# MoE layers of a hybrid decoder trunk: stored expert results cleared in advance, loaded two steps sooner, and the last two steps' results added on the chip

## The chip, the cores and the metric

The kernel runs on one core of a Trainium2 chip. The metric is the time of one execution on the device in microseconds (us). Each core has five engines: TensorE (PE; its weight loads are listed as PEld), VectorE (DVE), ScalarE (ACT), GpSimd (POOL) and SyncE (SP), which here only issues DMAs.

## What is computed

512 tokens of width 1024 in float32 pass through two layers, each with a mixer and a mixture of experts (MoE) in post-norm form, `x <- LN(alpha*x + mixer(x)); x <- LN(alpha*x + MoE(x))`. Layer 0 has an S5 and convolution mixer, layer 1 a sparse attention. The change is in the MoE, which is the same in both layers:

```python
def moe(x, router_w, router_b, w_gate, w_up, w_down, s_gate, s_up, s_down):
    scores = jax.nn.sigmoid(xt @ router_w)
    _, idx = lax.top_k(scores + router_b, TOP_K)          # 8 of 64 experts
    gate = jnp.take_along_axis(scores, idx, axis=1)
    gate = gate / gate.sum(-1, keepdims=True) * ROUTE_SCALE
    ...
    def expert_rows(args):
        tok, g, e = args
        xb = x_pad[tok]
        h = jax.nn.silu(xb @ w_gate[e]) * (xb @ w_up[e])  # 1024 -> 256
        return (h @ w_down[e]) * g[:, None]               # 256 -> 1024
    ...
    routed = jnp.zeros((n + 1, d), x.dtype).at[row_tok].add(y_rows.reshape(n_rows, d))[:n]
    shared = (jax.nn.silu(xt @ s_gate) * (xt @ s_up)) @ s_down
    return (routed + shared)
```

Each token's output is thus the sum of 8 gated expert rows and the shared expert's row; 512 x 8 = 4096 expert rows in all.

## The kernel before, in words

`program` calls `even_mixer`, `moe_layer` 0, `odd_mixer`, `moe_layer` 1. Each is a block with one instruction stream per engine; the streams wait for each other through semaphores only, and each stream runs in the order in which it is written. There is a barrier between blocks.

`moe_layer` has three stages.

*The start* (PE from L479, DVE from L708). The mixer's output projection (`out_project`), the first norm, the router and the shared expert run tile by tile (4 tiles of 128 tokens). SP loads constants and shared weights (L222 to L227), then stores each normed tile to `h_dram` (L229 to L231) as it comes, then the second norm's constants, and once the routing is known, the first experts' weights (L235 on). POOL fills tables, and gathers rows only after all four stores have landed (L329).

*The steps.* A step handles 128 rows. Three steps `k` = 0, 1, 2 make a round `t`; steps 0 and 1 serve one expert each, step 2 two experts with 64 rows each. POOL gathers the rows' inputs from `h_dram` (`gather`, L300), PE turns them (`rows_transposes`, L421), multiplies with gate and up weights (`gate_up`, L439 and L442), turns the hidden rows (L452) and multiplies with the down weights (`down`, L472 and L475). ACT and DVE scale one half each by the gates into `y[k]` (`scale`, L652 and L785), and POOL scatters `y[k]` to `y_dram`, row 8 x token + rank (`send`, L315). Places of a step that no token fills have an index beyond the bounds and are not written. Every step of a round but the last also starts weight loads on SP (L268 to L281). One step comes ahead of the rounds (t = -1, k = 2); the loop over `t` has a last round of its own, written out. Here there are 49 steps in each layer.

*The tail.* SP waits until all three steps of the last round are scattered (L250 to L253) and then loads all of `y_dram`, 16 loads of 1 MB, each two of the eight rows of 128 tokens, into `pieces`, 16 places in `wide`, `weights` and `xy` (L124, L283 to L286). Tile by tile, DVE adds rows 0 to 2 to `x` (`add_row`, L898), PE adds rows 3 to 7 in PSUM by matmuls with the identity (`row_sums`, L578, 10 matmuls, each listed as two records), DVE adds that sum (the "fold", L906) and runs the norm (L1001 to L1011). In layer 0, PE also turns the result into `g.xT` (`turn_output`, L587) for the next part, and SP loads the next part's `wide` weights when tile 0 is folded (L288). In layer 1 SP stores the tiles to `out` (L293).

## Time and profile before

| | us |
|---|---|
| median of 3 runs | 2124.73 |
| lowest, highest | 2122.98, 2125.33 |
| the profiled execution | 2123.23 |
| its span | 2121.2 |
| PE busy | 1990.8 (94%) |
| DVE busy | 746.5 (35%) |
| ACT busy | 400.1 (19%) |
| POOL busy | 394.7 (19%) |
| DMA, bytes moved | 566.01 MB, mean 267 GB/s |

The span runs from the first to the last instruction of the profiled execution; its time, 2123.23 us, holds 2 us more around it. Busy shares overlap, and matmuls are pipelined, so a busy PE is not one at its peak. Layer 0's MoE block runs from about 210 to 993 us, layer 1's from about 1341 to the end. A timeline's row merges neighbours of one kind: it gives the start of the first, the time from it to the end of the last, and their count; idle time ahead of it stands in brackets with what ended it. `PEclk` is the clock that TensorE was granted, as a share of 2.4 GHz (0.50 is 1.2 GHz).

### The profile page before, as it was taken

What the parts mean: (1) busy time and instruction counts of PE and PEld (TensorE: products, weight loads), DVE (VectorE), ACT (ScalarE), POOL (GpSimd) and SP (SyncE); (2) the same over time, 40 slices, a digit from 0 to 9 for tenths busy, and PEclk for the clock granted to TensorE, in tenths of its full rate; (3) what the DMA queues carried; (4) which work ended last, traced back from release to release, by engine and by line L of the source; (5) the groups of instructions that cost most, each with busy time, mean ns of one, the idle gap of its engine ahead of it and who ended that gap; (6) DMA issues with size and microseconds to landing.
All of it is one profiled execution on the core that took longest, in us unless ns stands there. A gap on an engine that the chain in (4) does not pass through costs nothing. (4 is left out here: it accounts for less than half of the span.)

```text
span 2121.2 us, 26424 instructions
## 1 busy us (share of the span) xinstructions
PE 1990.8 (94%) x8534; PEld 989.3 (47%) x8534; DVE 746.5 (35%) x1929; ACT 400.1 (19%) x890; POOL 394.7 (19%) x381
## 2 busy tenths in 40 slices
PE   8998998999999999978998898998999999999977
PEld 4553454444444444433446565554444444444433
DVE  3683352222222222216432566343222222222216
ACT  2103021111111111101002566111111111111110
POOL 0000200111111111100110778500111111111110
PEclk9999999999999999999998899999999999999998
DMA  6132245999999999958402000226899999999957
GB/s 227 11 53 113 111 190 212 400 407 412 406 409 388 412 396 386 401 229 352 78 0 80 1 2 2 105 77 266 334 407 402 417 406 411 399 412 400 406 220 332
DMA packets 107426, 566.01 MB, mean 267 GB/s; under 512 B 38625, under 2 KB 39393, under 8 KB 69089
## 3 DMA queue, kind: packets, MB, share of 16 engines
q1 hardware_dynamic: 79136, 497.99, 59.1%
q0 software_dynamic: 28224, 67.16, 8.1%
q8 instruction: 40, 0.66, 0.1%
q14 instruction: 26, 0.20, 0.0%
HBM read 539.78 MB, written 59.77 MB: 283 GB/s over the span
## 5 line engine op out<-in xcount | busy, mean ns | idle before, releaser
L439 PE MATMUL moe_bank<-moe_weights,moe_xgT 128*128 128x512 f32 x1024 | 457.0, 599 | 15.5 <-DMA moe_weights<-in_ex_weights 15.1
L439 PEld LDWEIGHTS moe_bank<-moe_weights,moe_xgT 128*128 128x128 f32 x1024 | 190.0, 190 | 232.2 <-issue 215.9
L315 POOL DMA_INDIRECT y<-moe_xy,moe_rows x98 | 98.6, 1006 | 945.2 <-DVE moe_idx L757 569.1
L777 DVE TENSOR_TENSOR moe_hid<-moe_sil,moe_bank 128x256 f32<-128x256 f32 x98 | 41.3, 421 | 661.1 <-ACT moe_sil L640 661.1
L472 PE MATMUL moe_bank<-moe_weights,moe_hidT 128*128 128x512 f32 x512 | 230.5, 593 | 0.0
L442 PE MATMUL moe_bank<-moe_weights,moe_xgT 128*64 128x512 f32 x512 | 226.6, 595 | 0.0
L442 PE MATMUL moe_bank<-wide,moe_xgT 128*64 128x512 f32 x512 | 226.6, 595 | 0.0
L640 ACT ACTIVATE moe_sil<-moe_bank 128x256 f32<-128x256 f32 x98 | 37.6, 383 | 657.4 <-PE moe_bank L439 456.0
L785 DVE TENSOR_SCALAR moe_xy<-moe_bank,moe_sgate 128x512 f32<-128x512 f32 x98 | 73.6, 751 | 219.5 <-PE moe_bank L472 142.1
L300 POOL DMA_INDIRECT moe_xy<-h,moe_idx x98 | 99.9, 1019 | 267.1 <-DVE moe_idx L757 239.5
L1847 POOL TENSOR_SCALAR att_prob<-att_prob,att_coef 128x128 f32<-128x128 f32 (+3 forms) x128 | 136.7, 1089 | 60.6 <-DVE att_coef L2015 37.8
L472 PEld LDWEIGHTS moe_bank<-moe_weights,moe_hidT 128*128 128x128 f32 x512 | 92.4, 191 | 93.4 <-issue 93.4
L421 PEld LDWEIGHTS moe_bank<-const_sb,moe_xy 128*128 128x128 f32 x784 | 100.6, 192 | 67.5 <-issue 51.6
L442 PEld LDWEIGHTS moe_bank<-moe_weights,moe_xgT 128*64 128x64 f32 x512 | 67.5, 137 | 128.8 <-issue 127.9
L652 ACT ACTIVATE moe_xy<-moe_bank,moe_sgate 128x512 f32<-128x512 f32 x98 | 67.3, 687 | 290.9 <-PE moe_bank L472 190.7
L348 PE MATMUL moe_bank<-wide,xT 128*128 128x512 f32 x256 | 113.7, 600 | 7.7 <-PEq L46 7.7
L475 PE MATMUL moe_bank<-moe_weights,moe_hidT 128*64 128x512 f32 x256 | 116.7, 598 | 1.9 <-ACT moe_hidT L644 1.9
L475 PE MATMUL moe_bank<-wide,moe_hidT 128*64 128x512 f32 x256 | 116.7, 598 | 0.0
L421 PE MATMUL moe_bank<-const_sb,moe_xy 128*128 128x128 f32 x784 | 107.5, 281 | 9.7 <-DMA moe_xy<-h,moe_idx 9.7
L348 PEld LDWEIGHTS moe_bank<-wide,xT 128*128 128x128 f32 x256 | 48.3, 193 | 65.0 <-issue 65.0
L1953 ACT ACTIVATE att_prob<-att_prob,att_low 128x128 f32<-128x128 f32 (+3 forms) x128 | 70.4, 551 | 33.7 <-DVE att_low L1979 33.6
L770 DVE COPY moe_xgT<-moe_bank 128x512 f32<-128x512 f32 x98 | 67.8, 692 | 18.4 <-PE moe_bank L421 18.0
(353 smaller groups left out, 2432.8 us busy)
## 6 DMA issues: line engine op xcount, KB each, us to landing
moe_weights<-in_ex_weights SPq DMA_DIRECT2D x96, 2048.0 KB, 19.6
moe_weights<-in_ex_weights SPq DMA_DIRECT2D x96, 1024.0 KB, 19.2
wide<-in_ex_weights SPq DMA_DIRECT2D x34, 2048.0 KB, 22.0
wide<-in_ex_weights SPq DMA_DIRECT2D x34, 1024.0 KB
moe_weights<-y SPq DMA_DIRECT2D x18, 1024.0 KB, 20.7
wide<-y SPq DMA_DIRECT2D x8, 1024.0 KB, 7.9
moe_xy<-y SPq DMA_DIRECT2D x6, 1024.0 KB, 27.0
oddin_win<-in_od_w_in_heads SPq DMA_DIRECT2D x1, 4288.0 KB, 18.7
```

What stands on the lines that cost most here:

```text
L300: pool.indirect_dma_start(out=xg[k], out_offset=None, in_=h_dram[0:SEQ, :], in_offset=IndirectOffsetOnAxis(ap=idx[k][:, 0:1], axis=0), bou ...
L315: pool.indirect_dma_start(out=y_dram[:, :], out_offset=IndirectOffsetOnAxis(ap=rows[k][:, 0:1], axis=0), in_=y[k], in_offset=None, bounds_ ...
L348: mm = pe.matmul(bout[n % 4][:, :], g.xT[:, k, i * P:(i + 1) * P], g.wide[:, k, h * 512:(h + 1) * 512], start=(k == 0), stop=(k == KC - 1))
L421: mm = pe.transpose(bX[n // 4][:, (n % 4) * P:(n % 4 + 1) * P], xg[k].rearrange("t (k c) -> t c k", c=KC)[:, n, :], c["ident"])
L439: mm = pe.matmul(bG[:, :], xgT[:, n, :], wgu[j][:, :, n, :], start=(n == 0), stop=(n == KC - 1))
L442: mm = pe.matmul(bG[HP * h:HP * h + HP, :], xgT[:, n, HP * h:HP * h + HP], wgu[2 + h][:, :, n, :], start=(n == 0), stop=(n == KC - 1))
L472: mm = pe.matmul(bY[half][:, :], hidT[:, n, :], wdn[j][:, n, cols], start=(n == 0), stop=(n == HC - 1))
L475: mm = pe.matmul(bY[half][HP * h:HP * h + HP, :], hidT[:, n, HP * h:HP * h + HP], wdn[2 + h][:, n, cols], start=(n == 0), stop=(n == HC - 1))
L770: dve.tensor_copy(xgT[:, 4:8, :].rearrange("p k t -> p (k t)"), bX[1][:, :]).then_inc(xT_v, 1)
L785: dve.tensor_scalar(y[k][:, 512:1024], bY[1][:, :], sgate[k][:, 0:1], None, ALU.mult).then_inc(y_v, 1)
L1847: pool.tensor_scalar(prob[n % 4][:, hb, 0:width], prob[n % 4][:, hb, 0:width], coef[n % 3][:, hb:hb + 1], None, ALU.mult).then_inc(scaled, 1)
L1953: act.activation(prob[k % 4][:, hb, 0:width], prob[k % 4][:, hb, 0:width], ACT.Exp, scale=-1.0, bias=low[k % 2][:, hb:hb + 1], accum_out=t ...
```

## The change

Four things change in `moe_layer`:

- Every row of `y_dram` is set to zero at the block's start: POOL clears 1024 columns of `weights` first of all (`zeros`), and SP writes them out in four DMAs of 4 MB (`clear_rows`), two ahead of the first `h` store, one after each of the next two. POOL waits for all four (`zeroed`) before its first scatter, SP before the first expert weights.
- The last round's steps 1 and 2 are not scattered. Their results stay in `y[1]` and `y[2]`. DVE makes eight 128x128 matrices of 0 and 1 (`where_last_steps_go`, into `xgT`, from the steps' token numbers), and PE adds the results to the sums of each tile through them (`last_steps`, 4 matmuls a tile).
- SP starts to load the stored rows once the last round's step 0 is scattered. The 16 places change so that each is free in time: the first five need nothing more (two lie in `g.xT`), loads 5 and 6 wait for the last `gate_up`, loads 7 on for the last `down`.
- DVE adds rows 0 to 3 instead of 0 to 2, for tile 0 three of them between its two last scalings; PE adds rows 4 to 7. Tile 0's row sum moves into the last round, right behind its last `down`. The next part's `wide` weights wait for two tiles' folds instead of one.

```diff
@@ -121,8 +121,15 @@
         pair = 2 * D
-        pieces = [a[:, q * pair:(q + 1) * pair].rearrange("p (r d) -> p r d", r=2)
-                  for a, n in ((wide, 4), (weights, 9)) for q in range(n)] + [xy[:, 2 * q:2 * q + 2, :] for q in range(3)]
+        flat_xT = g.xT[:].rearrange("p k t -> p (k t)")
+        two_rows = lambda a, q: a[:, q * pair:(q + 1) * pair].rearrange("p (r d) -> p r d", r=2)
+        pieces = [two_rows(flat_xT, 0), two_rows(flat_xT, 1), two_rows(wide, 3), two_rows(weights, 0),
+                  two_rows(weights, 1), two_rows(wide, 0), two_rows(wide, 1), two_rows(wide, 2),
+                  two_rows(weights, 2), two_rows(weights, 3), two_rows(weights, 4), two_rows(weights, 5),
+                  xy[:, 0:2, :], xy[:, 2:4, :], two_rows(weights, 6), two_rows(weights, 7)]
+        place = xgT
+        tok = s.sb("tok", [P, 2])
+        zeros = weights[:, 0:D]
@@ -147,7 +154,7 @@
         bout = bank[3:7]
-        ON_DVE = 3
+        ON_DVE, EARLY = 4, 3
@@ -173,6 +180,7 @@
         half_done, folded, stored = s.sem("half_done"), s.sem("folded"), s.sem("stored")
+        zeros_ready, zeroed, tok_ready, place_ready = s.sem("zeros_ready"), s.sem("zeroed"), s.sem("tok_ready"), s.sem("place_ready")
         turned, turned_a, turned_v = s.sem("turned"), s.sem("turned_act"), s.sem("turned_dve")
@@ -183,6 +191,9 @@
             sp.dma_start(spaces[j][:, 2 * KC * DE:per_slot], w["ex_weights"][layer, ds(e, 1), :, 2 * KC * DE:per_slot].rearrange("o p n -> p (o n)")).then_inc(dn_landed[j], 16)
+
+        def token_rows(i):
+            return y_dram[i * P * TOPK:(i + 1) * P * TOPK, :].rearrange("(t r) d -> t r d", r=TOPK)
@@ -226,11 +237,19 @@
+            def clear_rows(i):
+                sp.dma_start(token_rows(i), zeros.unsqueeze(1).to_broadcast([P, TOPK, D])).then_inc(zeroed, 16)
+
+            sp.wait_ge(zeros_ready, 1)
+            clear_rows(0)
             for i in range(NT):
+                if i + 1 < NT:
+                    clear_rows(i + 1)
                 norm1.wait_tile(sp, i)
...
             sp.wait_ge(out_done, 2 * NT)
+            sp.wait_ge(zeroed, 16 * NT)
             sp.wait_ge(owners, 2)
@@ -247,12 +266,25 @@
             for t, last in rounds(sp):
+                b = step_no(t, 0)
                 if last:
-                    for k in range(STEPS):
-                        sp.wait_ge(scattered[k], 16 * uses(t, k) + 16)
+                    sp.wait_ge(xT_done, b + STEPS)
+                    sp.sem_inc(loading, 1)
+                    for k in (2, 1):
+                        sp.wait_ge(scattered[k], 16 * uses(t, k))
                         sp.sem_inc(loading, 1)
+                    sp.wait_ge(scattered[0], 16 * uses(t, 0) + 16)
+                    sp.sem_inc(loading, 1)
+                    for n in range(4 * NT):
+                        if n == 5:
+                            sp.wait_ge(gu_done, b + STEPS)
+                            sp.sem_inc(loading, 1)
+                        if n == 7:
+                            sp.wait_ge(dn_done, b + STEPS)
+                            sp.sem_inc(loading, 1)
+                        i, j = n // 4, n % 4
+                        sp.dma_start(pieces[n], token_rows(i)[:, 2 * j:2 * j + 2, :]).then_inc(landed[i][j], 16)
                     continue
-                b = step_no(t, 0)
@@ -280,12 +312,8 @@
-            for i in range(NT):
-                tokens = y_dram[i * P * TOPK:(i + 1) * P * TOPK, :].rearrange("(t r) d -> t r d", r=TOPK)
-                for j in range(4):
-                    sp.dma_start(pieces[4 * i + j], tokens[:, 2 * j:2 * j + 2, :]).then_inc(landed[i][j], 16)
             if out is None:
-                sp.wait_ge(folded, 2)
+                sp.wait_ge(folded, 4)
                 g.load_wide(sp, w["od_w_in_heads"].rearrange("(p c) f -> p c f", c=KC)[:, :, 0:D])
@@ -316,6 +344,7 @@
+            pool.memset(zeros, 0.0).then_inc(zeros_ready, 1)
             for k in range(STEPS):
@@ -331,12 +360,14 @@
             gather_next(-1, STEPS - 1)
+            pool.wait_ge(zeroed, 16 * NT)
             send(-1, STEPS - 1)
...
                         gather_next(t, k)
-                    send(t, k)
+                    if not last or k == 0:
+                        send(t, k)
@@ -475,6 +506,35 @@
                 mm.then_inc(dn_done, 1)
+
+            def stored_rows(i, first, final):
+                for r in range(ON_DVE, TOPK):
+                    pe.wait_ge(landed[i][r // 2], 16)
+                    for h in range(2):
+                        mm = pe.matmul(bsum[i % 2][h][:, :], c["ident"], pieces[4 * i + r // 2][:, r % 2, h * 512:(h + 1) * 512],
+                                       start=(first and r == ON_DVE), stop=(final and r == TOPK - 1))
+                return mm
+
+            def last_steps(i, first, final):
+                pe.wait_ge(place_ready, 1)
+                for q in range(2):
+                    for h in range(2):
+                        mm = pe.matmul(bsum[i % 2][h][:, :], place[:, NT * q + i, :], y[1 + q][:, h * 512:(h + 1) * 512],
+                                       start=(first and q == 0), stop=(final and q == 1))
+                return mm
+
+            def row_sums(i, steps_made=None):
+                if i >= 2:
+                    pe.wait_ge(folded, 2 * (i - 1))
+                if i == 0:
+                    stored_rows(i, True, False)
+                    pe.wait_ge(y_a, steps_made)
+                    pe.wait_ge(y_v, steps_made)
+                    mm = last_steps(i, False, True)
+                else:
+                    last_steps(i, True, False)
+                    mm = stored_rows(i, False, True)
+                mm.then_inc(half_done, 1)
@@ -568,16 +628,8 @@
                     down(t, k)
-
-            def row_sums(i):
-                if i >= 2:
-                    pe.wait_ge(folded, 2 * (i - 1))
-                for r in range(ON_DVE, TOPK):
-                    pe.wait_ge(landed[i][r // 2], 16)
-                    for h in range(2):
-                        mm = pe.matmul(bsum[i % 2][h][:, :], c["ident"], pieces[4 * i + r // 2][:, r % 2, h * 512:(h + 1) * 512],
-                                       start=(r == ON_DVE), stop=(r == TOPK - 1))
-                mm.then_inc(half_done, 1)
+                    if last and k == STEPS - 1:
+                        row_sums(0, step_no(t, k) + 1)
@@ -588,7 +640,7 @@
-            for i in range(NT - 1):
+            for i in range(1, NT - 1):
                 row_sums(i)
@@ -783,6 +835,21 @@
                 dve.tensor_scalar(y[k][:, 512:1024], bY[1][:, :], sgate[k][:, 0:1], None, ALU.mult).then_inc(y_v, 1)
+
+            def where_last_steps_go(b):
+
+                dve.wait_ge(gu_done, b + 1)
+                for q in range(2):
+                    dve.tensor_copy(tok[:, q:q + 1], idx[1 + q][:, 0:1]).then_inc(tok_ready, 1)
+                dve.wait_ge(tok_ready, 2)
+                for q in range(2):
+                    for i in range(NT):
+                        made = dve.tensor_scalar(place[:, NT * q + i, :], c["slotno"], float(P * i - 1), tok[:, q:q + 1], ALU.add, ALU.is_equal)
+                made.then_inc(place_ready, 1)
+
+            def add_row(i, r):
+                dve.wait_ge(landed[i][r // 2], 16)
+                adds.link(dve, dve.tensor_tensor(g.x[:, i, :], g.x[:, i, :], pieces[4 * i + r // 2][:, r % 2, :], ALU.add))
@@ -889,16 +956,17 @@
                         one_hot(*later(t + 1, k, 1))
+                    if last and k == 1:
+                        where_last_steps_go(step_no(t, k + 1))
                     scale(t, k)
+                    if last and k == 1:
+                        for r in range(EARLY):
+                            add_row(0, r)
...
-            def add_row(i, r):
-                dve.wait_ge(landed[i][r // 2], 16)
-                adds.link(dve, dve.tensor_tensor(g.x[:, i, :], g.x[:, i, :], pieces[4 * i + r // 2][:, r % 2, :], ALU.add))
-
             for i in range(NT):
-                for r in range(ON_DVE):
+                for r in range(0 if i else EARLY, ON_DVE):
                     add_row(i, r)
```

SP's queue in the first MoE block, from the loads of the shared weights to the second norm's constants; `y<-moe_weights` is a clear, `h<-x_sb` a store of a tile. Before:

```order
L226 DMA moe_weights<-in_sh_w_up 128x2048
L227 DMA moe_weights<-in_sh_w_down 128x2048
L231 DMA h<-x_sb 128x1024 x4
L988 DMA moe_ln_g<-in_ln_g 128x1024
L989 DMA moe_ln_b<-in_ln_b 128x1024
```

And with the change:

```order
L237 DMA moe_weights<-in_sh_w_up 128x2048
L238 DMA moe_weights<-in_sh_w_down 128x2048
L241 DMA y<-moe_weights 1024x1x1024 x2
L249 DMA h<-x_sb 128x1024
L241 DMA y<-moe_weights 1024x1x1024
L249 DMA h<-x_sb 128x1024
L241 DMA y<-moe_weights 1024x1x1024
L249 DMA h<-x_sb 128x1024 x2
L1056 DMA moe_ln_g<-in_ln_g 128x1024
L1057 DMA moe_ln_b<-in_ln_b 128x1024
```

The four stores stood together; now two clears stand ahead of the first store and one each ahead of the second and the third.

DVE in the last round and the tail of the second MoE block: L777 (L829) makes the last step's hidden rows, L785 (L837) are the last two scalings, L898 (L852) are row adds, L906 (L974) the fold of tile 0. Before:

```order
L777 TENSOR_TENSOR moe_hid<-moe_sil,moe_bank 128x256
L785 TENSOR_SCALAR moe_xy<-moe_bank,moe_sgate 128x512 x2
L995 MEMSET moe_ln_eps 128x1
L898 TENSOR_TENSOR x_sb<-x_sb,wide 128x1024 x3
L906 TENSOR_TENSOR x_sb<-x_sb,moe_bank 128x512 x2
```

And with the change:

```order
L829 TENSOR_TENSOR moe_hid<-moe_sil,moe_bank 128x256
L843 CAST moe_tok<-moe_idx 128x1 x2
L847 TENSOR_SCALAR moe_xgT<-const_sb,moe_tok 128x128 x8
L837 TENSOR_SCALAR moe_xy<-moe_bank,moe_sgate 128x512
L852 TENSOR_TENSOR x_sb<-x_sb,xT 128x1024 x3
L837 TENSOR_SCALAR moe_xy<-moe_bank,moe_sgate 128x512
L1063 MEMSET moe_ln_eps 128x1
L852 TENSOR_TENSOR x_sb<-x_sb,xT 128x1024
L974 TENSOR_TENSOR x_sb<-x_sb,moe_bank 128x512 x2
```

The matrices come ahead of the scaling of step 1, and three row adds between the two scalings.

PE in the tail of the second MoE block: L578 (L514) are matmuls of stored rows with the identity, L522 those of `y[1]` and `y[2]` with the 0/1 matrices. Before:

```order
L475 MATMUL moe_bank<-wide,moe_hidT 64x512
L578 MATMUL moe_bank<-wide,const_sb 128x512 x10
L578 MATMUL moe_bank<-moe_weights,const_sb 128x512 x20
L578 MATMUL moe_bank<-moe_xy,const_sb 128x512 x10
L42 UNCONDITIONAL_BRANCH
```

And with the change:

```order
L506 MATMUL moe_bank<-wide,moe_hidT 64x512
L514 MATMUL moe_bank<-wide,const_sb 128x512 x4
L514 MATMUL moe_bank<-moe_weights,const_sb 128x512 x4
L522 MATMUL moe_bank<-moe_xy,moe_xgT 128x512 x8
L514 MATMUL moe_bank<-wide,const_sb 128x512 x8
L522 MATMUL moe_bank<-moe_xy,moe_xgT 128x512 x4
L514 MATMUL moe_bank<-moe_weights,const_sb 128x512 x8
L522 MATMUL moe_bank<-moe_xy,moe_xgT 128x512 x4
L514 MATMUL moe_bank<-moe_weights,const_sb 128x512 x8
L42 UNCONDITIONAL_BRANCH
```

40 matmuls become 48, 12 a tile; only in tile 0 do the stored rows come first.

## Rows read from the trace of the kernel before

**Rows 1.** The page's second part, 40 slices of 53 us, busy or granted tenths

```profile
PE   8998998999999999978998898998999999999977
...
PEclk9999999999999999999998899999999999999998
```

**Rows 2.** Timeline of PE, tail of B: start, us, engine, line, operation, [idle before <-releaser]

```profile
2054.84 0.61 PE L475 MATMUL moe_bank<-moe_weights,moe_hidT 128*64 128x512 f32 x1 [0.97 <-ACT moe_hidT L644]
...
2057.91 0.59 PE L475 MATMUL moe_bank<-wide,moe_hidT 128*64 128x512 f32 x1
...
2070.91 11.91 PE L578 MATMUL moe_bank<-wide,const_sb 128*128 128x512 f32 x20 [12.41 <-DMA wide<-y]
...
2082.66 10.46 PE L578 MATMUL moe_bank<-moe_weights,const_sb 128*128 128x512 f32 x24
```

**Rows 3.** Timeline of POOL and of SP, tail of B

```profile
2044.49 0.99 POOL L315 DMA_INDIRECT y<-moe_xy,moe_rows  x1 [10.62 <-ACT moe_xy L652]
...
2063.55 1.92 SPq L286 DMA_DIRECT2D wide<-y  x4
```

**Rows 4.** Timeline of DVE, tail of B

```profile
2050.47 0.42 DVE L777 TENSOR_TENSOR moe_hid<-moe_sil,moe_bank 128x256 f32<-128x256 f32 x1 [6.80 <-ACT moe_sil L640]
...
2053.68 0.75 DVE L785 TENSOR_SCALAR moe_xy<-moe_bank,moe_sgate 128x512 f32<-128x512 f32 x1 [2.79 <-PE moe_bank L472]
...
2068.46 3.75 DVE L898 TENSOR_TENSOR x_sb<-x_sb,wide 128x1024 f32<-128x1024 f32 x3 [9.17 <-DMA wide<-y]
...
2082.93 1.28 DVE L906 TENSOR_TENSOR x_sb<-x_sb,moe_bank 128x512 f32<-128x512 f32 x2 [10.73 <-PE moe_bank L578]
...
2088.97 3.73 DVE L898 TENSOR_TENSOR x_sb<-x_sb,moe_weights 128x1024 f32<-128x1024 f32 x3
...
2111.38 1.28 DVE L906 TENSOR_TENSOR x_sb<-x_sb,moe_bank 128x512 f32<-128x512 f32 x2
```

**Rows 5.** Stretches in B: length, busy us of PE, PEld, DVE, ACT, POOL, then PEclk, DMA share, GB/s

```profile
2060.00:2065.00 5.00, 0.00 (x0) 0.00 (x0) 0.00 (x0) 0.00 (x0) 0.98 (x1) 0.85 0.36 111
...
2070.00:2075.00 5.00, 4.09 (x5) 1.85 (x6) 2.17 (x2) 0.00 (x0) 0.00 (x0) 0.50 1.01 428
```

**Rows 6.** Timelines of POOL, SP and DVE, tail of A

```profile
917.99 0.99 POOL L315 DMA_INDIRECT y<-moe_xy,moe_rows  x1 [10.61 <-ACT moe_xy L652]
...
937.06 1.88 SPq L286 DMA_DIRECT2D wide<-y  x4
...
954.77 1.28 DVE L906 TENSOR_TENSOR x_sb<-x_sb,moe_bank 128x512 f32<-128x512 f32 x2 [9.09 <-PE moe_bank L578]
...
984.31 1.28 DVE L906 TENSOR_TENSOR x_sb<-x_sb,moe_bank 128x512 f32<-128x512 f32 x2 [0.66 <-PE moe_bank L578]
```

**Rows 7.** DMA issues in 2043 to 2046 and in 916 to 921: count, us to landing

```profile
y<-moe_xy,moe_rows POOLq DMA_INDIRECT x1, 5.9
...
y<-moe_xy,moe_rows POOLq DMA_INDIRECT x1, 4.5
```

**Rows 8.** Timeline of DVE in A's routing

```profile
293.60 0.34 DVE L834 TENSOR_SCALAR moe_spilt<-const_sb,moe_spill_slot,moe_spills 64x125 f32<-64x125 f32 x1
```

**Rows 9.** Start of A, timelines of SP and POOL, stretches and landing of L231; B's first gather

```profile
231.52 47.27 SPq L231 DMA_DIRECT2D h<-x_sb  x4
...
296.76 0.36 SPq L182 DMA_DIRECT2D wide<-in_ex_weights  x1
...
311.76 1.20 POOL L300 DMA_INDIRECT moe_xy<-h,moe_idx  x1 [84.46 <-DVE moe_idx L757]
...
1440.89 1.12 POOL L300 DMA_INDIRECT moe_xy<-h,moe_idx  x1 [83.08 <-DVE moe_idx L757]
...
220.00:230.00 10.00, 10.00 (x24) 4.37 (x23) 3.55 (x6) 1.58 (x2) 7.30 (x6) 1.00 0.46 196
...
240.00:250.00 10.00, 10.00 (x43) 5.93 (x42) 5.51 (x8) 0.29 (x1) 0.00 (x0) 1.00 0.14 54
...
DMA to landing us min/median/max: 2.6/2.6/2.9
```

## Prediction

> **What bounds the kernel now.** I read the page first: PE's busy row stands at 8 and 9 nearly everywhere, but falls to 7 in the 19th slice (954 to 1007 us), over the end of the first MoE layer, and in the last two; in the last the clock falls to 8 too [rows 1]. Call the layers A (ends near 990 us) and B (ends with the program). The matmuls inside the steps are untouched, so the question is the two tails, from the last step's end to the output, and what the clears do at each layer's start.
>
> The tail of B, in order of time, from the timelines. The last `down` ends on PE at 2057.91 + 0.59 = 2058.5 and its successor, the first row sum, starts at 2070.91, after 12.4 us in which PE waited for a DMA [rows 2]. The 16 loads of stored rows begin at 2063.55, when the last scatter has landed [rows 3]. VectorE's first row add starts at 2068.46, 4.9 us after the first issue [rows 4], PE's first sum, which needs the second load, 7.4 us after it. So loads land at +4.9, +7.4 and, at 428 GB/s, every 1.05 MB / 428 = 2.45 us behind that [rows 5]. PE begins at half clock, 1.2 GHz [rows 5], so the first tile's 20 matmul records take until 2082.66, 11.75 us; at full clock 24 records take 10.46 us, 0.436 each [rows 2], so they would have taken 8.7. VectorE folds that sum in at 2082.93, and from there it never waits: its next tile begins at 2088.97, and from that tile's fold, 3.77 later, to the last one at 2111.38 are two tiles of 9.32 us, of which three adds are 3.73 [rows 4]. DMA runs ahead of it. **The tail is therefore load start, first two or so loads, one tile of PE, then four tiles of VectorE.** A is the same with its own times [rows 6].
>
> **The change, part by part.**
>
> *Loads start sooner.* Two of the last three scatters go; the loads wait for the one of the last round's step 0. That scatter is in the trace: issued 2044.49 and landed 5.9 us later, 2050.4; in A 917.99 + 4.5 = 922.5 [rows 3, 6, 7]. What ran beside it is unchanged. So the first load is issued at 2050.5 instead of 2063.55 (13.1 us sooner) and at 922.6 instead of 937.06 (14.5). The later waits open no hole: load 5 needs the last gate-and-up product, done when VectorE multiplies its result at 2050.47 [rows 4]; load 7 needs the last `down`, 2058.5, while the seven loads ahead of it occupy the DMA for 17.2 us.
>
> *PE's first tile.* It now needs loads 2 and 3 (rows 4 to 7), at +9.8 and +12.3: 2060.3 and 2062.8 in B, 932.4 and 934.9 in A. The last `down` ends at 2058.5 in B, 14.0 after the step-0 scatter's issue, and so at 932.0 in A; PE idles 1.8 and 0.4 us instead of 12.4. In the slice in which it had stopped at 2058.5, up to 2065, the clock's mean was still 0.85 [rows 5], so a 2 us pause should keep 2.4 GHz. Work: 8 matmuls of stored rows and 4 with the 0/1 matrices, 24 records instead of 20, 24 x 0.436 = 10.5 us. The sum is ready at 2070.8 and 942.9, VectorE folds 0.1 later: 2070.9 against 2082.93, 12.0 sooner; 943.0 against 954.77, 11.8 sooner [rows 4, 6].
>
> *VectorE's tail.* Tile 0's three early adds run from 2055.4 to 2059.1 in B; they put its last scaling 0.6 us late, which nobody feels, since PE is in the stored rows until 2067.3. The fourth add is done long before the fold. Tiles 1 to 3 carry a fourth add each, 1.24 us: 3.7 us later. B: the last fold moves from 2111.38 to 2070.9 + 6.04 (fold and norm of tile 0) + 4.97 (four adds) + 2 x 10.56 = 2103.0, 8.4 us sooner; what follows is as before. PE needs 24 records a tile, 10.46 plus, I guess, 0.2 of waiting between loads, so its last sum comes at 2102.8: the two engines are now level, and neither has slack. A: 943.0 + 6.04 + 4.97 + 21.1 = 975.1 by VectorE; PE also turns one output there (0.9 us), 975.8; fold at 975.9 against 984.31, again 8.4 sooner [rows 6]. The wide weights of the next part now wait for two tiles' folds; that is about 955.4 (943.0 + 6.04 + 4.97 + 1.3), where tile 0's was 956.05 (954.77 + 1.28), and the queue ahead of them is shorter, so they land no later.
>
> *The 0/1 matrices.* VectorE makes them between 2050.9 and its scaling at 2053.68, an idle stretch of 2.8 us [rows 4]. Eight comparisons at no more than 0.34 (the 64x125 form with two scalars [rows 8]) and two casts of one column, which I put at 0.15, are 3.0 us at most, so 0.2 late at worst. The scaling then ends at 2054.6; PE's last `down`, which it holds up, started at 2054.84, 0.97 idle for ScalarE's copy of the hidden rows [rows 2]: nothing. Without that cover PE would wait the 0.2.
>
> *The clears.* Each layer writes 16.8 MB of zeros from SP's queue, two clears before the first `h` store, two between stores. Behind them stand the four stores, the second norm's constants, and, by a new wait, the first expert weights; POOL's gathers wait for the stores. No large write is in the trace. The nearest is the `h` store: at a share of 0.14 of the engines it moves 54 GB/s, so 386 at full share; but alone it lands in 2.6 us, which vouches for no more than 202 GB/s [rows 9]. I take 386, because loads of the same rows with the same spacing run at 428. Then in A the input loads end near 225 (a share of 0.46 of 220 to 230 [rows 9]); clears 0 and 1 take until 247, clear 2 until 259, clear 3 (issued at 246) until 271 with the stores between, before the last store is issued at 278.5 (four issues in 47.27 us from 231.52). The first expert load is issued at 296.76 and the first gather at 311.76 [rows 9]. Cost 0. In B the first gather is at 1440.89, 1129.1 later, and I shift the rest by as much. At 202 GB/s, 18.9 MB last 93.6 us from 225: 318.6, the gather 6.9 late in each layer, 13.8 together. Weights would be issued 17 us late and still land before PE takes them. POOL's memset of the zeros, as many elements as a row add of 1.24 us, is first on its queue and holds SP no longer than that.
>
> The Trainium skill ("DMA: Bandwidth & Descriptors", Latency and other measured facts) speaks against this: copies with a row pitch that is a large power of two fell to 207 GB/s at 512 KiB and 103 at 4 MiB. The pitch here is 32 KiB per partition, below its table, and loads at that pitch reach 428 in this trace. By 207 GB/s the sum would be some 9 us worse, an estimate from that page.
>
> *Sum:* -8.4 - 8.4 = -16.8 us. The profiled execution took 2123.2, so 2106.4; the median of the runs is 1.5 higher, so 2107.9. I say 2107.
>
> **Rivals.**
> - *Same path, cold PE (0.07).* If PE's clock falls in its short pause or loads 2 and 3 come late, the first tile costs the 3.0 us again that it loses before: -10.8 in both layers together, 2113. For it: the clock did fall within a few us of idling. Against: 1.8 us is short.
> - *More than I say (0.05).* The load start moves 27.6 us in all, and the added adds take back 7.4: up to -20, 2103, if VectorE's early adds and PE's warm start overlap better than the rows let me see.
> - *The loads do not start sooner (0.05).* If the step-0 scatter lands 5 to 6 us later than it did [rows 7], PE idles long enough to start cold: 8.4 - 5.5 - 3 is nothing in either layer, 2123. Against it: nothing that the change touches shares the DMA with that scatter.
> - *Slow clears, the other side (0.05).* One mechanism: writes of rows 32 KiB apart under 195 GB/s hold the last `h` store, and with it the first gather, 8.4 us or more in each layer (18.9 MB / 95.2 us = 198 GB/s; I say 195 to be clear of it); from there the gain is gone. At 160 GB/s the 118 us end at 343 in A, 31 late, and B as much: 2123.2 - 16.8 + 62 = 2168. The page's pitch rule would be such a mechanism, and at its 207 it stops short of that point.
>
> **How the numbers follow.** About 0.2%, 4.2 us, can be told from no change. Forecast 0.78, cold PE 0.07, more 0.05, no sooner start 0.05, slow clears 0.05 (0.04 slower, 0.01 near same). The range goes from 2103 (the better case) to 2113 (cold PE); it leaves out the last two. Faster: 0.78 + 0.07 + 0.05, and a little of the next, 0.91; same 0.05; slower 0.04.
>
> **What the profile will show.** Right: SP's first load of stored rows near 922.6 and in B 13 us sooner relative to the last step; PE's pause after the last `down` under 3 us and the clock row without its dip; VectorE's period 10.5 us a tile; the clears at about 390 GB/s and ended before the last `h` store, and the first gathers as far from each layer's start as before. Wrong: a first gather waiting for the stores; a PE stretch at 1.2 GHz in the first row sum; folds that wait for PE by over 1 us per tile; a hole in the loads before load 7.

## The result, and the profile after

The changed kernel takes 2104.28 us (median of 6 runs, 2102.48 to 2110.54), the kernel before, run beside it, 2123.86 (6 runs). The ratio is 0.9914 with a 95% interval of 0.9905 to 0.9924: 18.3 us less. The forecast was 2107, with a range of 2103 to 2113. The profiled execution took 2104.37 us with a span of 2102.6, 18.6 below the span of before.

The page's first lines and three rows of its 40 slices, for the changed kernel:

```profile
span 2102.6 us, 26532 instructions
...
PE 1997.5 (95%) x8566; PEld 994.1 (47%) x8566; DVE 760.7 (36%) x1957; ACT 400.5 (19%) x890; POOL 392.4 (19%) x379
...
PEclk9999999999999999999998899999999999999999
DMA  6133955999999999987402000656899999999977
...
HBM read 539.78 MB, written 91.23 MB: 300 GB/s over the span
```

The clock's dip in the last slice [rows 1] is gone. The kernel writes 31.5 MB more: 33.6 MB of zeros, less four scatters of 0.52 MB.

**The tail of B.** Timelines of POOL and SP (start, us, engine, line, operation):

```profile
2034.00 0.98 POOL L343 DMA_INDIRECT y<-moe_xy,moe_rows  x1 [10.62 <-ACT moe_xy L704]
...
2039.98 0.81 SPq L286 DMA_DIRECT2D xT<-y  x2
2040.84 0.42 SPq L286 DMA_DIRECT2D wide<-y  x1
2041.31 1.06 SPq L286 DMA_DIRECT2D moe_weights<-y  x2
2042.49 5.93 SPq L286 DMA_DIRECT2D wide<-y  x3
2048.47 1.86 SPq L286 DMA_DIRECT2D moe_weights<-y  x4
```

The step-0 scatter is issued at 2034.00 and the loads begin 5.98 us behind it, where they began 19.06 behind it before [rows 3]. The wait ahead of the sixth load holds nothing up: it goes out at 2042.49. SP does stop ahead of the eighth (load 7, counted from 0), for 4.7 us: the row of three `wide<-y` is stretched because its last one is issued only at 2048.10, when the last `down` ends. DMA does not run dry meanwhile, since the seven loads ahead still occupy it: its share stays at 1.01 from 2045 to 2055.

VectorE's timeline there:

```profile
2040.32 0.21 DVE L843 CAST moe_tok<-moe_idx 128x1 f32<-128x1 uint32 x2
2040.57 1.66 DVE L847 TENSOR_SCALAR moe_xgT<-const_sb,moe_tok 128x128 f32<-128x128 f32 x8
2043.19 0.75 DVE L837 TENSOR_SCALAR moe_xy<-moe_bank,moe_sgate 128x512 f32<-128x512 f32 x1 [0.97 <-PE moe_bank L503]
2044.82 3.79 DVE L852 TENSOR_TENSOR x_sb<-x_sb,xT 128x1024 f32<-128x1024 f32 x3 [0.87 <-DMA xT<-y]
...
2060.50 1.28 DVE L974 TENSOR_TENSOR x_sb<-x_sb,moe_bank 128x512 f32<-128x512 f32 x2 [9.96 <-PE moe_bank L522]
...
2071.56 1.29 DVE L974 TENSOR_TENSOR x_sb<-x_sb,moe_bank 128x512 f32<-128x512 f32 x2
...
2092.72 1.28 DVE L974 TENSOR_TENSOR x_sb<-x_sb,moe_bank 128x512 f32<-128x512 f32 x2
```

The matrices cost 1.9 us and VectorE still waits 0.97 for PE behind them. The three early adds end at 2048.61, and the last scaling, ready when the last `down` ended at 2048.0, starts at 2048.64. The folds come at 2060.50, 2071.56, 2082.14 and 2092.72; only the first waits, the second follows at 11.06 and the last two at 10.58 each.

PE's timeline, and below it stretches with their length, busy us of PE, PEld, DVE, ACT and POOL, then PEclk, DMA share and GB/s:

```profile
2049.83 3.70 PE L514 MATMUL moe_bank<-wide,const_sb 128*128 128x512 f32 x8 [1.82 <-DMA wide<-y]
2053.36 3.60 PE L514 MATMUL moe_bank<-moe_weights,const_sb 128*128 128x512 f32 x8
2056.80 7.03 PE L522 MATMUL moe_bank<-moe_xy,moe_xgT 128*128 128x512 f32 x16
...
2084.26 7.03 PE L514 MATMUL moe_bank<-moe_weights,const_sb 128*128 128x512 f32 x16
```

```profile
2050.00:2055.00 5.00, 5.00 (x12) 2.21 (x13) 0.54 (x1) 0.00 (x0) 0.00 (x0) 1.00 1.01 424
...
2080.00:2085.00 5.00, 5.00 (x13) 2.25 (x12) 4.85 (x7) 0.00 (x0) 0.00 (x0) 1.00 0.76 309
2085.00:2090.00 5.00, 5.00 (x13) 2.25 (x12) 4.84 (x5) 0.29 (x1) 0.00 (x0) 1.00 0.28 111
```

PE waits 1.82 us instead of 12.41 [rows 2], keeps its 2.4 GHz, and then has no gap. The loads thin out in 2080 to 2085, more than one tile ahead of the last fold.

**The tail of A.** SP's and VectorE's timelines:

```profile
921.84 0.80 SPq L286 DMA_DIRECT2D xT<-y  x2
...
984.59 1.27 SPq L1726 DMA_DIRECT2D oddin_win<-in_od_w_in_heads  x2
```

```profile
942.36 1.28 DVE L974 TENSOR_TENSOR x_sb<-x_sb,moe_bank 128x512 f32<-128x512 f32 x2 [8.61 <-PE moe_bank L522]
...
974.86 1.28 DVE L974 TENSOR_TENSOR x_sb<-x_sb,moe_bank 128x512 f32<-128x512 f32 x2
```

Measured from the issue of the step-0 scatter, which removes what differs between executions ahead of it, both tails read so (us; "end" is the next part's first load in A, the span's end in B):

```
                 before                          after
A  load start    19.07                            4.10
   folds         36.78  46.87  56.37  66.32      24.62  35.97  46.54  57.12
   end           76.56                           66.85   (-9.7)
B  load start    19.06                            5.98
   folds         38.44  48.25  57.57  66.89      26.50  37.56  48.14  58.72
   end           76.71                           68.60   (-8.1)
```

17.8 of the span's 18.6 us are in the two tails. The remaining 0.8 lies outside them, and by so much or more the stretches between differ from one execution to the next.

**The clears.** SP's timeline at A's start, POOL's first gather, and stretches with the columns as above:

```profile
212.41 7.13 SPq L241 DMA_DIRECT2D y<-moe_weights  x2
230.33 0.34 SPq L249 DMA_DIRECT2D h<-x_sb  x1
...
260.87 16.73 SPq L249 DMA_DIRECT2D h<-x_sb  x2
...
295.57 0.37 SPq L190 DMA_DIRECT2D wide<-in_ex_weights  x1
...
310.55 1.19 POOL L328 DMA_INDIRECT moe_xy<-h,moe_idx  x1 [84.06 <-DVE moe_idx L809]
```

```profile
220.00:230.00 10.00, 10.00 (x25) 4.42 (x24) 4.61 (x7) 1.58 (x2) 6.49 (x5) 1.00 1.01 419
230.00:240.00 10.00, 10.00 (x36) 5.29 (x35) 2.28 (x4) 0.60 (x1) 0.00 (x0) 1.00 1.02 421
...
260.00:270.00 10.00, 10.00 (x31) 4.97 (x30) 2.22 (x3) 0.60 (x1) 0.00 (x0) 1.00 0.67 277
```

Zeros are written at 419 to 421 GB/s and are over at about 267, reckoned from the 277 GB/s of the stretch 260 to 270. POOL's gather is released by VectorE's list of indices, not by the stores, and comes 101.8 us after the layer's first load, against 101.3 before [rows 9]; in B 99.78 against 99.79.

### The profile page after: what moved, and what is told of

It reads as the page before. It is cut to its first block and busy times, and to the rows that moved or that the text cites. A ratio compares the mean times of both kernels' runs of the same rounds, so it can differ in the third digit from the quotient of the medians.

```text
span 2102.6 us, 26532 instructions
## 1 busy us (share of the span) xinstructions
PE 1997.5 (95%) x8566; PEld 994.1 (47%) x8566; DVE 760.7 (36%) x1957; ACT 400.5 (19%) x890; POOL 392.4 (19%) x379
## 5 line engine op out<-in xcount | busy, mean ns | idle before, releaser
L829 DVE TENSOR_TENSOR moe_hid<-moe_sil,moe_bank 128x256 f32<-128x256 f32 x98 | 41.3, 421 | 658.0 <-ACT moe_sil L692 658.0
L837 DVE TENSOR_SCALAR moe_xy<-moe_bank,moe_sgate 128x512 f32<-128x512 f32 x98 | 73.5, 750 | 208.3 <-PE moe_bank L503 138.5
## 6 DMA issues: line engine op xcount, KB each, us to landing
moe_weights<-in_ex_weights SPq DMA_DIRECT2D x96, 2048.0 KB, 19.4
wide<-in_ex_weights SPq DMA_DIRECT2D x34, 2048.0 KB, 21.8
```

The lines of the kernel that those rows point to most:

```text
L837: dve.tensor_scalar(y[k][:, 512:1024], bY[1][:, :], sgate[k][:, 0:1], None, ALU.mult).then_inc(y_v, 1)
```

## The experiments

The first four ran on one chip beside 25 runs of the kernel before (2121.9 us), the next four on another beside 8 (2124.3), the last three on a third beside 7 (2123.3). Ratios are to those runs, with 95% intervals.

**The clears alone.** The kernel before, with the clears and their three waits (SP ahead of the expert weights, POOL ahead of its first scatter, SP for the zeros) and nothing else of the change:

```diff
+            sp.wait_ge(zeros_ready, 1)
+            clear_rows(0)
             for i in range(NT):
+                if i + 1 < NT:
+                    clear_rows(i + 1)
                 norm1.wait_tile(sp, i)
...
+            sp.wait_ge(zeroed, 16 * NT)
```

> The kernel before with the clears and their waits alone; every scatter and the old tail stay. Theory (the clears are hidden): they run at some 420 GB/s, end before the last h store, and the time is that of the kernel before, 2124, within 2 us. Rival (the clears cost something, and the tail gave more than its rows say): between 2 and 10 us slower than before. In the trace the distance from each block's start to its first gather tells them apart: 101.3 us in A in both kernels by the theory.

2123.28 us (10 runs), 1.0005 (0.9995 to 1.0015). The first gathers stand 101.44 and 99.78 us behind each layer's first load, where they stand 101.30 and 99.79 before. The times alone leave room for 3 us, the low end of the rival; the distances to the first gather do not. 33.6 MB of writes are hidden.

**The loads late again, all else of the change kept.** SP waits for the last `down` ahead of the first load:

```diff
                     sp.wait_ge(scattered[0], 16 * uses(t, 0) + 16)
                     sp.sem_inc(loading, 1)
+                    sp.wait_ge(dn_done, b + STEPS)
+                    sp.sem_inc(loading, 1)
```

> The changed kernel, but SP waits for the last down before its first load of stored rows; no scatter comes back. Theory (the gain is the load start and, with it, a warm PE): loads start 8.1 us later in B and 9.8 in A, PE idles about 10 us and starts its first tile at 1.2 GHz, 1.5 to 3 us more; first folds come 10 to 12 us later, about 22 us in all, 2126, no faster than before. Rival (the gain comes from two scatters less and from the local adds, whatever the start): under 2112.

2127.11 us (10 runs), 1.0022 (1.0011 to 1.0033): by the ratio 4.7 us slower than before, as the theory had it. PE's timeline and one stretch in B:

```profile
2066.55 6.16 PE L516 MATMUL moe_bank<-wide,const_sb 128*128 128x512 f32 x8 [10.04 <-DMA wide<-y]
```

```profile
2065.00:2070.00 5.00, 3.45 (x4) 1.51 (x5) 2.24 (x4) 0.00 (x0) 0.00 (x0) 0.50 1.01 426
```

Eight records, begun at a granted clock of 0.50 (0.85 in the stretch 2070 to 2075), take 6.16 us, where the changed kernel's take 3.70. The first fold comes 23.06 us after the load start in B and 22.36 in A, against 20.52 in both with the change: 2.5 and 1.8 us for PE's cold start. The loads of this kernel still start 14.1 us behind the step-0 scatter, 4.9 sooner than in the kernel before, and yet its last folds come 2.5 (B) and 2.7 us (A) later, by the longer way from load start to last fold. So everything else of the change costs time; the whole gain comes from the earlier load start and from what it spares PE.

**The kernel before with a warm PE.** 13 matmuls of constants into a bank that nobody reads, ahead of the first row sum:

```diff
+            for n in range(13):
+                pe.matmul(bG[:, :], c["ident"], c["causal"], start=True, stop=True)
             for i in range(NT - 1):
                 row_sums(i)
```

> The kernel before with 13 matmuls without a use (identity by the causal table, into a free bank, 11.3 us at full clock) in PE's pause of 12.4 us ahead of the first row sum. Theory (part of the gain is the clock): the first tile runs at 2.4 GHz; it is then held only by its loads, and the first fold comes 2.5 us sooner in B (2080.4 where it was 2082.9) and 0.8 in A (953.9 for 954.8), 3.3 us in all: 2120.6. Rival (the loads set the first fold, the clock nothing): no change.

A miss: 2123.46 us (10 runs), 1.0004 (0.9994 to 1.0015), no gain where 3.3 us were expected. The extra matmuls did warm PE; a stretch of this kernel in B, where before has 0.50 [rows 5], and its timelines of PE and VectorE:

```profile
2070.00:2075.00 5.00, 4.08 (x9) 1.73 (x10) 1.68 (x2) 0.00 (x0) 0.00 (x0) 1.00 1.02 428
```

```profile
2081.74 1.98 PE L578 MATMUL moe_bank<-moe_weights,const_sb 128*128 128x512 f32 x4 [1.28 <-DMA moe_weights<-y]
2084.23 7.13 PE L578 MATMUL moe_bank<-moe_weights,const_sb 128*128 128x512 f32 x16 [0.50 <-DMA moe_weights<-y]
...
2104.11 7.13 PE L578 MATMUL moe_bank<-moe_xy,const_sb 128*128 128x512 f32 x16 [0.45 <-DMA moe_xy<-y]
```

```profile
2080.57 1.28 DVE L908 TENSOR_TENSOR x_sb<-x_sb,moe_bank 128x512 f32<-128x512 f32 x2 [8.86 <-PE moe_bank L578]
2091.47 1.28 DVE L908 TENSOR_TENSOR x_sb<-x_sb,moe_bank 128x512 f32<-128x512 f32 x2 [1.13 <-PE moe_bank L578]
2101.41 1.28 DVE L908 TENSOR_TENSOR x_sb<-x_sb,moe_bank 128x512 f32<-128x512 f32 x2 [0.65 <-PE moe_bank L578]
2111.35 1.28 DVE L908 TENSOR_TENSOR x_sb<-x_sb,moe_bank 128x512 f32<-128x512 f32 x2 [0.66 <-PE moe_bank L578]
```

From the load start the first fold is 1.9 us sooner in B (17.45 against 19.38) and 0.65 in A, but in B each later one now waits for PE, and PE for a load. The last three folds are 9.94 apart, and four loads of 1.05 MB at 421 GB/s take 9.96. VectorE's own 9.32 a tile is shorter. In the kernel before, the cold start let the loads run 1.9 us ahead; from there VectorE took 28.45 us to the last fold (9.81 and twice 9.32), where three tiles of loads take 29.9, so 1.4 of the 1.9 were used up. The last fold comes 48.2 us after the load start here, and 47.8 before. The old tail had two limits within half a us of each other, the loads' and VectorE's behind a cold PE, and taking one away shows the other.

The loads' limit shows without the extra matmuls too. In A of the kernel before the last fold already waits 0.66 us for PE [rows 6], and PE for a load:

```profile
977.07 7.13 PE L578 MATMUL moe_bank<-moe_xy,const_sb 128*128 128x512 f32 x16 [0.20 <-DMA moe_xy<-y]
```

In the kernel with the clears alone, whose tail is the old one, B's first fold came 0.7 us sooner behind its load start than in the profile of before; its last fold then waited 1.01 for PE and came at 48.1.

**Zeros twice.** In the changed kernel each clear is followed by one of as many bytes into a spare buffer, and both waits count all eight:

```diff
                 sp.dma_start(token_rows(i), zeros.unsqueeze(1).to_broadcast([P, TOPK, D])).then_inc(zeroed, 16)
+                sp.dma_start(spare_rows(i), zeros.unsqueeze(1).to_broadcast([P, TOPK, D])).then_inc(zeroed, 16)
...
```

> The changed kernel with every clear written twice, the second time to a spare array of the same size that nobody reads: 33.6 MB a layer instead of 16.8. Theory (clears run at 420 GB/s and have slack up to the first gather): with the stores they take 85 us from where the input loads end, to about 307 in A where the first gather is at 310.5, and just in time in B; the first weights are issued some 12 us later and still land early. 0 to 3 us in all: 2104 to 2107. Rival (the clears have little slack): the first gather and all behind it 8 us or more late in each layer, over 2118.

2109.07 us (4 runs), 0.9929 (0.9911 to 0.9947), some 3 us above the changed kernel by the ratios, the top of the 0 to 3 expected; the two intervals overlap. SP's and POOL's timelines:

```profile
234.16 17.61 SPq L253 DMA_DIRECT2D h<-x_sb  x1
...
309.81 0.36 SPq L190 DMA_DIRECT2D wide<-in_ex_weights  x1
```

```profile
1432.95 1.12 POOL L332 DMA_INDIRECT moe_xy<-h,moe_idx  x1 [84.99 <-DMA h<-x_sb]
```

The queue backs up, an `h` store stands 17.6 us in it, and B's first gather is now released by the store, 2.8 us late (A's 1.3). Twice the bytes at 420 GB/s take as long as the same bytes at 210, so this run stands for the slow-clears rival at 210 GB/s, just short of the 195 at which it would lose 8 us a layer. Reckoned as in the prediction, 35.7 MB from 225 end at 310, just where A's first gather stands: the margin was as wide as reckoned, to a few us, and the change uses half of it (42 of 85 us).

**Three and five rows on VectorE instead of four.** The second kernel has 5 where this one has 3:

```diff
-        ON_DVE, EARLY = 4, 3
+        ON_DVE, EARLY = 3, 3
```

> The changed kernel with rows 0 to 2 on VectorE and 3 to 7 on PE, as before the change. Theory (PE and VectorE are level at four rows each): PE has 28 records, 12.2 us, a tile; first fold 1.75 us later, the other three folds at 12.2 us instead of 10.6, so VectorE waits 1.6 us a tile for PE; 6 us in B, 7 in A: 2117. Rival (loads or VectorE bound the tail, PE has slack): under 2 us slower, or faster by up to 7.

> The changed kernel with rows 0 to 4 on VectorE and 5 to 7 on PE. Theory: first fold 1.7 us sooner, since PE has 20 records ahead of it, then VectorE's period 11.8 us instead of 10.6 and no wait for PE: 2.0 us a layer, 2108. Rival (PE bounds the tail): faster than the changed kernel.

Three: 2115.57 us (5 runs), 0.9959 (0.9945 to 0.9973). Five: 2108.25 us (4 runs), 0.9928 (0.9911 to 0.9944). A tile's end on VectorE's timeline, first with three, then with five:

```profile
2088.71 1.29 DVE L974 TENSOR_TENSOR x_sb<-x_sb,moe_bank 128x512 f32<-128x512 f32 x2 [2.73 <-PE moe_bank L514]
```

```profile
2084.55 1.28 DVE L974 TENSOR_TENSOR x_sb<-x_sb,moe_bank 128x512 f32<-128x512 f32 x2
```

With three, PE has 28 records a tile and B's period is 12.02. The later folds in B wait 2.25, 2.73 and 2.73 us for PE, more than the 1.6 expected, because with three adds VectorE's own tile is 9.3 us and not 10.6. The first fold is 1.7 later in A and not later in B, where PE has row 3 to add during the 1.8 us that it waits in the changed kernel. With five VectorE is the bound at 11.84, no fold after the first waits, and the first is only 0.5 (A) to 1.0 us (B) sooner, since PE now waits for loads there. Four, at 10.58, is where the two engines are level, as the prediction had it.

**Seven rows of tile 0 on VectorE.** In the changed kernel VectorE idles 9.96 us ahead of the first fold while PE works through rows 4 to 7. Here VectorE adds rows 0 to 6 of tile 0, and PE does its last-step products and row 7:

```diff
-        ON_DVE, EARLY = 4, 3
+        ON_DVE, EARLY = (7, 4, 4, 4), 3
...
                 if i == 0:
-                    stored_rows(i, True, False)
                     pe.wait_ge(y_a, steps_made)
                     pe.wait_ge(y_v, steps_made)
-                    mm = last_steps(i, False, True)
-                else:
-                    last_steps(i, True, False)
-                    mm = stored_rows(i, False, True)
+                last_steps(i, True, False)
+                mm = stored_rows(i, False, True)
...
```

> The changed kernel with tile 0 shared out otherwise: VectorE, idle for 8.6 and 10 us ahead of the first fold, adds seven of its rows, PE row 7 alone, and PE takes the kept results first. Tiles 1 to 3 stay at four and four. Theory (the tail is first fold plus VectorE's four tiles at 10.6): first fold 5.7 us sooner in B and 4.4 in A, PE catches up by 0.9 at tile 1, last folds 4.8 and 4.4 sooner, 2095. Rival (the loads bound the tail): the last tile's loads set its fold, under 2 us gained.

2094.89 us (4 runs), 0.9866 (0.9848 to 0.9883). VectorE's and PE's timelines in B:

```profile
2053.01 1.29 DVE L971 TENSOR_TENSOR x_sb<-x_sb,moe_bank 128x512 f32<-128x512 f32 x2 [0.68 <-PE moe_bank L514]
...
2065.04 1.29 DVE L971 TENSOR_TENSOR x_sb<-x_sb,moe_bank 128x512 f32<-128x512 f32 x2 [1.00 <-PE moe_bank L514]
...
2086.20 1.29 DVE L971 TENSOR_TENSOR x_sb<-x_sb,moe_bank 128x512 f32<-128x512 f32 x2
```

```profile
2057.80 7.13 PE L514 MATMUL moe_bank<-wide,const_sb 128*128 128x512 f32 x16 [1.46 <-DMA wide<-y]
```

The first fold comes 5.5 us sooner after the scatter than with the change (21.02 against 26.50), the last 4.5 sooner: tile 1's sum costs 1.00, because PE waits 1.46 for a load of that tile. In A the last fold gained 2.9 where 4.4 were expected: the scatter landed 1.6 us later than in the changed kernel's profile. That the median came out at the 2095 expected is partly luck.

**Tile 1's halves exchanged on top of that.** PE takes rows 0 to 3 of tile 1, which land first, and VectorE rows 4 to 7:

```diff
-        ON_DVE, EARLY = 4, 3
+        ON_PE, EARLY = (range(7, 8), range(0, 4), range(4, 8), range(4, 8)), 3
...
```

> The version with seven rows of tile 0 on VectorE (2094.9 measured), and in tile 1 PE takes rows 0 to 3 and VectorE rows 4 to 7, since PE waited 1.5 us there for load 6 and VectorE then 0.7 to 1.0 us for PE, while loads 4 and 5 had long landed. Theory: both waits go, about 1 us a layer, 2093. Rival (the waits fall elsewhere): no change.

2096.08 us (4 runs), 0.9874 (0.9857 to 0.9891), where the kernel without the exchange had 0.9866: no gain, a miss. PE's timeline, tiles 2 and 3 in B:

```profile
2064.53 7.13 PE L514 MATMUL moe_bank<-moe_weights,const_sb 128*128 128x512 f32 x16 [1.12 <-DMA moe_weights<-y]
...
2075.46 7.13 PE L514 MATMUL moe_bank<-moe_weights,const_sb 128*128 128x512 f32 x16 [0.36 <-DMA moe_weights<-y]
```

Tile 1's wait is gone, and in B PE waits for loads one tile later instead. The last fold in B comes 48.0 us after the load start, with the seven rows alone 48.2, with the change 52.7. 48 is also the length of the kernel before with a warm PE. There and with the exchange PE's last 16 records, 7.1 us, wait for the fifteenth load and begin 41.0 and 40.8 us after the load start; that is the loads' own limit. With the seven rows alone the limit is nearly met: the last fold waits for nothing, and PE's last sum was ready only 0.3 us ahead of it.

**Repeats, the three versions side by side.** The seven-row kernel, the exchanged one and the changed kernel, each as above, in one series:

> The version with seven rows of tile 0 on VectorE, once more. By its profile the two tails are 4.5 and 2.4 us shorter than the changed kernel's, by its first runs it is 9 us faster; from the rows I expect 7 to 9 us under the changed kernel.

> The version that also swaps rows in tile 1, once more. By its profile 1.5 us less than the one above in A's tail and 0.4 in B's, by its first runs 1 us more; theory: 1 to 2 us less; rival: the same within 1 us, then the swap is worth nothing that can be measured.

> The changed kernel once more, as it is, beside the two versions below on one chip. 0.991 of the kernel before by its first runs.

Seven rows: 2094.37 us, 0.9869 (0.9852 to 0.9885). Exchanged: 2094.71, 0.9863 (0.9847 to 0.9880). Changed kernel: 2103.20, 0.9912 (0.9896 to 0.9929). Four runs each. Seven rows beat the changed kernel by 9 us and the kernel before by some 28; the exchange makes no difference that can be told. These executions also show how the step-0 scatter's landing varies, and what it moves (A, us from its issue):

```
                  load start   first fold   last fold
changed           4.10         24.62        57.12
changed, again    5.74         26.18        58.68
seven rows        5.69         20.58        54.25
seven rows, again 3.41         20.46        52.97
```

In the changed kernel the whole tail follows the load start. With seven rows the first fold does not, since it hangs on PE and ScalarE, and the last does only through PE's wait for tile 1's load (1.48 us with the loads at 5.69): with the loads at 3.41 no fold after the first waits, and 20.46 plus three periods is what is left.

## Why the prediction was right

**Load start.** Forecast 13.1 us sooner in B and 14.5 in A; measured 13.08 and 14.97. The loads start 5.98 us (B) and 4.10 us (A) behind the step-0 scatter, which lands 5.9 us (B) and 4.0 us (A) after its issue, against 5.9 and 4.5 before [rows 7]. That the whole gain hangs on this step is shown by the late-start kernel. The wait ahead of load 7 opened no hole in the transfers, as argued, though SP itself stood still for 4.7 us.

**PE's first tile.** Forecast waits of 1.8 and 0.4 us, a warm clock, and first folds 12.0 and 11.8 sooner. Measured: 1.82 and less than 0.1 (the trace lists no wait), a clock of 1.00, and 11.94 and 12.16. PE's cold start in the new tail costs 2.5 us in B and 1.8 in A (late-start kernel), where 3.0 stood for it: the cold-PE rival would have given 4.3 us back, not 6. Its 3.0 was read in B and put on A unread: in A of the kernel before the first 20 records took 10.1 us, 1.4 over the 8.7 of a warm PE.

**VectorE's period.** Forecast 10.56 a tile and 3.7 us later over three tiles; measured 10.58 and, from first to last fold in B, 32.22 against 28.45, 3.77. That PE and VectorE are level there is shown by the kernels with three and five rows. In A 3.4 were forecast and 2.96 measured, by two errors that partly cancel: PE's turning and 0.2 of waits between loads, 0.8 in all, did not show as waits, and B's 6.04 for fold and norm of tile 0 stood where A takes 6.3. With that and the early landing of this execution's scatter A gained 9.2 us at the last fold instead of 8.4; in the repeat, where the scatter landed 1.6 later, 7.6.

**0/1 matrices and early adds.** The matrices were forecast at 3.0 us at most, 0.2 late; they took 1.87 and were not late. The early adds put B's last scaling 0.6 us late, as forecast, and PE reaches its results only at 2056.80.

**The clears.** Forecast 386 GB/s and an end at 271; 420 and 267, cost 0 (clears alone: between 0.05% less and 0.15% more, and first gathers in their old places). The smallest row pitch for which the Trainium skill ("DMA: Bandwidth & Descriptors", Latency and other measured facts) gives a slow copy is 512 KiB, at 207 GB/s. At 32 KiB this trace shows no such slowing: writes run at 419 to 421 GB/s, at the rate of the reads.

**The step that was wrong.** "DMA runs ahead of it", and with it "load start, first two or so loads, one tile of PE, then four tiles of VectorE" as the one length of the old tail, in A as in B. Its own row for A spoke against it: there the last fold waited 0.66 for PE [rows 6]. The prediction never set four loads against a tile: 9.96 us against VectorE's 9.32. The old tail was as long by its loads as by its engines, and the warm-PE kernel shows that the 3.0 us of cold start, taken as a loss that the change gives back, cost the old tail nothing that the runs can tell. The sum came out all the same, because the old tail's 47.8 us from load start to last fold were read from the trace and the new tail is 52.7 by VectorE, at a period longer than the loads' 9.96: the difference needs no cause for the old length. Of the B gain of 8.2 us, 13.1 is load start, and -4.9 the longer way from there to the last fold. That the wrong step did no harm is luck: had VectorE's new tail come out under some 48 us from the load start, as it nearly does with the seven rows, the loads would have set its end. With the wrong picture an edit that only warms PE would have been sold at 6 us; it was expected at 3.3 and gave nothing.

**What stays open.** Why unchanged parts and the scatter's landing (3.4 to 6.2 us) differ by a us or two from one execution to the next. And how much is left in the seven-row kernel, which in B stands at VectorE's and the loads' limits at once: giving PE fewer of the last tile's late rows was not tried.

## What to carry to other kernels

Write a pipelined tail once for each resource, as its first item plus so many periods, and compare the ends: here the loads (9.96 us a tile) gave 48.2 us, and VectorE (9.32) behind a cold PE gave 47.8. In B's timeline only the first fold waited, so the loads' limit did not show there; A's last fold, with a wait of 0.66, was the sign of it. When work moves from one engine to another, balance the first tile apart from the steady ones: it has no predecessor to hide behind, and moving its rows to the engine that idled there was worth another 9 us. Clearing a buffer in advance, so that fewer writes have to be awaited, is free as long as its bytes fit into a stretch in which DMA idles; doubling the bytes tells how much room is left.

## What the runs showed of the hardware

- Writes of 4 KB rows from one zeroed row per partition, rows of a partition 4 KB apart and partitions 32 KiB apart, run at 419 to 421 GB/s, 4.2 MB a transfer; the reads of the same rows in B at 419 to 428. The `h` stores had vouched for 202 to 386 [rows 9].
- PE, idle for 10.0 us, began at a granted clock of 0.50, and its first 8 records took 6.16 us instead of 3.70; idle for 1.8 us it kept 1.00. In the kernel before the mean clock of the stretch 2060 to 2065, which begins 1.5 us after PE stopped, was 0.85 [rows 5].
- Large transfers waiting in the queue delay SP itself: behind four clears the issue of one `h` store took 17.6 us, where with the change, behind two, the first takes 0.34 in A and 1.38 in B.
